# Scores of the short branch as three one-pass products of split q and k

## The reference: one layer with two attention branches

```
h = rms_norm(x, norm_g)                       # x: 1 x 4096 x 1024, float32
qa, ka, va, za, qb, kb, vb, zb, ga, gb = split(h @ w_in)
qa, ka = partial_rope(qa), partial_rope(ka)   # first 16 of 64 channels of a head
ya = swa_sink_attention(qa, ka, va, sinks) * silu(za)      # 8 q heads, 2 kv heads
yb = chunked_relpos_attention(qb, kb, vb, bias) * silu(zb) # 8 heads
merged = sigmoid(ga + b0) * (ya @ w_br_a) + sigmoid(gb + b1) * (yb @ w_br_b)
out = rms_norm(x + merged @ w_out, final_g)
```

## Time and profile before

| | us |
|---|---|
| median of 3 runs | 3419.65 (3418.62 to 3423.51) |
| the profiled execution, its own time | 3421.02 |
| its span in the profile | 3419.2 |
| TensorE busy | 3342.8 (98%) |
| VectorE busy | 1482.7 (43%) |
| ScalarE busy | 1422.4 (42%) |
| GpSimd busy | 1309.1 (38%) |
| mean granted TensorE clock | 0.999 |

### The profile page before, as it was taken

How to read it: one execution, slowest core, us unless ns; L and a number is a source line. 1 busy time by engine, 2 the same in 40 slices (tenths; PEclk the granted TensorE clock), 3 DMA queues, 4 the chain that set the end, 5 groups by cost and what they waited for, 6 DMA issues and landing times.

```text
span 3419.2 us, 48305 instructions
## 1 busy us (share of the span) xinstructions
PE 3342.8 (98%) x16328; PEld 2496.7 (73%) x16328; DVE 1482.7 (43%) x3097; ACT 1422.4 (42%) x2969; POOL 1309.1 (38%) x1087
## 2 busy tenths in 40 slices
PE   7999999999999999999999999999999999999998
PEld 6667876678766787667876678766787667876676
DVE  4662355513555135551355513555135551355512
ACT  4443444434444344443444434444344443444432
POOL 3334542344423454234542345423454234542244
PEclk9999999999999999999999999999999999999999
DMA  4212431124311242112421225211242112521123
GB/s 156 62 62 88 171 99 50 62 87 167 99 51 62 86 169 97 55 61 83 173 93 55 61 83 173 93 56 62 81 172 94 56 61 83 173 94 55 56 82 116
DMA packets 97782, 319.53 MB, mean 93 GB/s; under 512 B 9984, under 2 KB 26624, under 8 KB 95360
## 3 DMA queue, kind: packets, MB, share of 16 engines
q1 hardware_dynamic: 97536, 316.34, 28.5%
HBM read 299.52 MB, written 16.78 MB: 93 GB/s over the span
## 4 chain that ended last, share of the span: by engine, by line
PE 84%; issue 7%; DVE 5%; POOL 2%; ACT 1%; DMA 0%; DVEq 0%; POOLq 0%; SPq 0%; ACTq 0%
PE acc L909 16%; PE acc L911 14%; PE acc L910 14%; PE ps_o L1004 6%; PE ps_pt L973 5%; PE sc L953 3%; PE sc L909 3%; PE sc L911 3%; PE sc L910 3%; POOL w_lo L755 2%; PE sc L944 2%; PE sc L853 2%; PE sc L852 2%; PE sc L851 2%; PE sc L876 1%
## 5 line engine op out<-in xcount | busy, mean ns | idle before, releaser
L755 POOL TENSOR_TENSOR w_lo<-w_raw,w_hi 128x512 fp32r<-128x512 f32 x928 | 1210.3, 1310 | 2048.1 <-ACT w_hi L1058 2046.9
L909 PE MATMUL acc<-h_hi,w_hi 128*128 128x512 f32 x2432 | 1012.1, 416 | 15.5 <-DVE q L1316 15.5
L911 PE MATMUL acc<-h_hi,w_lo 128*128 128x512 f32 x2432 | 953.1, 392 | 0.0
L910 PE MATMUL acc<-h_lo,w_hi 128*128 128x512 f32 x2432 | 950.4, 391 | 0.0
L1058 ACT ACTIVATE w_hi<-w_raw 128x512 fp32r<-128x512 f32 x928 | 574.4, 625 | 393.1 <-DMA w_raw<-w 118.0
L909 PEld LDWEIGHTS acc<-h_hi,w_hi 128*128 128x128 f32 x2432 | 456.4, 188 | 228.5 <-issue 146.5
L911 PEld LDWEIGHTS acc<-h_hi,w_lo 128*128 128x128 f32 x2432 | 456.4, 188 | 101.7
L910 PEld LDWEIGHTS acc<-h_lo,w_hi 128*128 128x128 f32 x2432 | 458.1, 188 | 75.4
L1146 ACT ACTIVATE probs_b<-sc,negm 128x640 f32<-128x640 f32 x256 | 202.9, 794 | 390.3 <-DVE negm L1263 390.2
L1153 ACT ACTIVATE probs_t<-ps_pt 128x512 f32<-128x512 f32 (+1 forms) x272 | 150.7, 554 | 264.7 <-PE ps_pt L973 264.7
L1288 DVE SCALAR_TENSOR_TENSOR part<-th,sc 128x512 f32<-128x512 f32 x64 | 43.9, 686 | 467.9 <-PE sc L911 467.7
(11 more groups left out here) (140 smaller groups left out, 3916.4 us busy)
## 6 DMA issues: line engine op xcount, KB each, us to landing
w_raw<-w SPq DMA_DIRECT2D x464, 512.0 KB, 3.5
rows<-x SPq DMA_DIRECT2D x36, 512.0 KB, 7.4
xt<-x_t SPq DMA_DIRECT2D x16, 1024.0 KB, 10.0
out<-rows SPq DMA_DIRECT2D x32, 512.0 KB, 2.8
x_in<-x SPq DMA_DIRECT2D x28, 512.0 KB, 5.5
cs<-rope_tab SPq DMA_DIRECT2D x8, 512.0 KB, 4.3
bias<-near SPq DMA_DIRECT2D x1, 1024.0 KB, 13.5
g_out<-final_g SPq DMA_DIRECT2D x1, 512.0 KB, 11.6
```

Of the source, the lines that this page charges most:

```text
L755: pool.tensor_tensor(w_lo[n % 2][:, c], w_raw[n % 2][:, c], w_hi[n % 2][:, c].bitcast(FP32), ALU.subtract).then_inc(w_split, 1)
L909: pe.matmul(dst[:, :], hi, src_hi[:, k, :], start=begin, stop=False)
L910: pe.matmul(dst[:, :], hi, src_lo[:, k, :], start=False, stop=False)
L911: mm = pe.matmul(dst[:, :], lo, src_hi[:, k, :], start=False, stop=end)
```

## The change

q and k of branch A are kept as a rounded part and a remainder, both float32r (`q_a_hi`, `q_a_lo`, `k_a_hi`, `k_a_lo`), and the scores are three products in place of one float32 product. The two heads alternate within each term. To make the parts, the rope gets two further operations: after the sum (`rope_sum`) ScalarE rounds it (`rope_split`), and in a new step `rope_out` VectorE subtracts (`rope_done`). The rotated sine part goes to a buffer of its own, `pre_rot`, and the sum stays in `pre`. `q` of branch B becomes the single buffer `q_b`; branch A's q and the input buffer `x_in1` share the last two slots of `th`.

```
 lead:
-             v[0], [*v[1], ("rope_in", 0)], v[2], [("rope", 0), *v[3]], [("turn_v", 0), *k4[0]], ...
+             [*v[0], ("rope_out_k", 0)], [*v[1], ("rope_in", 0)], v[2], [("rope", 0), *v[3]],
+             [("turn_v", 0), *k4[0], ("rope_out", 0)], ...
 fill:
             fill[at_ + 3] = [("rope", s), *fill[at_ + 3]]
+            fill[at_ + 4] = [*fill[at_ + 4], ("rope_out", s)]

 GpSimd, keep_k:
-  pool.tensor_copy(k_a[:, 0:P], k_a[:, BLK:BLK + P]).then_inc(kept, 1)
+  pool.tensor_copy(k_a_hi[:, 0:P], k_a_hi[:, BLK:BLK + P].bitcast(FP32))
+  pool.tensor_copy(k_a_lo[:, 0:P], k_a_lo[:, BLK:BLK + P].bitcast(FP32)).then_inc(kept, 1)

 TensorE, scores of branch A:
-  for hh in range(2):
-      rows_ = slice(HD * hh, HD * hh + HD)
-      mm = pe.matmul(score_tile(s, hh, t)[:, c:A_KEYS], q[n % 2][rows_, t * P:(t + 1) * P],
-                     k_a[rows_, t * P + c:t * P + A_KEYS], start=True, stop=True)
+  terms = ((q_a_hi, k_a_hi), (q_a_lo, k_a_hi), (q_a_hi, k_a_lo))
+  for i, (q_part, k_part) in enumerate(terms):
+      for hh in range(2):
+          rows_ = slice(HD * hh, HD * hh + HD)
+          mm = pe.matmul(score_tile(s, hh, t)[:, c:A_KEYS], q_part[rows_, t * P:(t + 1) * P],
+                         k_part[rows_, t * P + c:t * P + A_KEYS], start=i == 0, stop=i == 2,
+                         skip_group_check=True)

 ScalarE, steps rope and rope_k (it had nothing in them):
+  act.wait_ge(rope_sum, b * NROPE + (ROPE_NO[step] + 1))
+  if kind == "rope_k" and not first:
+      wait_kept(act, b, "keep_k", PAIRS - 1)
+  act.activation(roped(kind)[0], pre[:, :], ACT.Copy).then_inc(rope_split, 1)

 VectorE, steps rope and rope_k, then rope_out and rope_out_k:
-  dve.tensor_tensor(dst, bank(step)[:, :], cs[:, 1, :], ALU.mult).then_inc(free(step), 1)
+  dve.tensor_tensor(pre_rot[:, :], bank(step)[:, :], cs[:, 1, :], ALU.mult).then_inc(free(step), 1)
   ...
-  dve.tensor_tensor(dst, pre[:, :], dst, ALU.add).then_inc(rope_done, 1)
+  dve.tensor_tensor(pre[:, :], pre[:, :], pre_rot[:, :], ALU.add).then_inc(rope_sum, 1)
+  dve.wait_ge(rope_split, b * NROPE + (no + 1))
+  dve.tensor_tensor(lo, pre[:, :], hi.bitcast(FP32), ALU.subtract).then_inc(rope_done, 1)
```

More of the change, by code:

```diff
@@ L154, in block_plan @@
     lead += [*tile("k", 0), q[0], [*q[1], ("rope_in_k", 0)], q[2], [("rope_k", 0), *q[3]],
-             v[0], [*v[1], ("rope_in", 0)], v[2], [("rope", 0), *v[3]], [("turn_v", 0), *k4[0]], *k4[1:], *tile("q", 4)]
+             [*v[0], ("rope_out_k", 0)], [*v[1], ("rope_in", 0)], v[2], [("rope", 0), *v[3]], [("turn_v", 0), *k4[0], ("rope_out", 0)], *k4[1:], *tile("q", 4)]
     for t in range(TT):
@@ L383, in program @@
     v_b = sb("v_b", [P, 2 * TT, PAIRS * P])
-    k_a = sb("k_a", [P, P + BLK])
+    k_a_hi = sb("k_a_hi", [P, P + BLK], FP32R)
+    k_a_lo = sb("k_a_lo", [P, P + BLK], FP32R)
     v_a = sb("v_a", [P, 1 + TT, P])
-    q_at = off[0]
-    q = [sb(f"q{i}", [P, BLK]) for i in range(2)]
+    q_b = sb("q_b", [P, BLK])
     z0 = sb("z0", [P, BLK])
@@ L411, in program @@
     pre_hi = at("pre_hi", [P, BLK], FP32R, y_lo_at + 4 * BLK * 7)
+    pre_rot = at("pre_rot", [P, BLK], FP32, y_lo_at + 4 * BLK * 6)
     bias = sb("bias", [P, 9, A_KEYS])
     x_in0_at = off[0]
-    x_in = [sb("x_in0", [P, D]), at("x_in1", [P, D], FP32, q_at)]
+    x_in0 = sb("x_in0", [P, D])
     probs_a = [at("probs_a0", [P, TT, A_KEYS], FP32, pa_at), at("probs_a1", [P, TT, A_KEYS], FP32, x_in0_at)]
@@ L418, in program @@
     cs = sb("cs", [P, 2, BLK])
+    th_at = off[0]
     th = sb("th", [P, 2 * AHEAD, BLK])
+    late_at = th_at + 4 * BLK * (2 * AHEAD - 2)
+    q_a_hi = at("q_a_hi", [P, BLK], FP32R, late_at)
+    q_a_lo = at("q_a_lo", [P, BLK], FP32R, late_at + 4 * BLK)
+    x_in = [x_in0, at("x_in1", [P, D], FP32, late_at)]
     gate = sb("gate", [P, BLK])
@@ L490, in program @@
     rope_cos = sem("rope_cos")
+    rope_sum = sem("rope_sum")
+    rope_split = sem("rope_split")
     rope_done = sem("rope_done")
@@ L633, in ring, with roped @@
         return probs_t[(FIRST_TURN if first else TURN)[turn][0] % RING]
+    def roped(kind):
+        if kind.endswith("_k"):
+            return k_a_hi[:, P:P + BLK], k_a_lo[:, P:P + BLK]
+        return q_a_hi[:, :], q_a_lo[:, :]
     def wait_kept(eng, b, kind, s):
@@ L727, in _ @@
             pool.memset(mhalf[:, :], -0.5).then_inc(zeroed, 1)
-            pool.memset(k_a[:, 0:P], 0.0).then_inc(zeroed, 1)
             pool.memset(v_a[:, 0, :], 0.0).then_inc(zeroed, 1)
@@ L731, in _ @@
             pool.memset(v_b[:, 0:TT, :], 0.0).then_inc(zeroed, 1)
-            pool.wait_ge(zeroed, 5)
+            pool.wait_ge(zeroed, 4)
             def rsqrt(which, t, n, got, got_count, mid, done, count):
@@ L826, in _ @@
             turn_rstd(0)
-            pe.wait_ge(zeroed, 5)
+            pe.wait_ge(zeroed, 4)
             def token_products(b, n, c):
@@ L952, in scores @@
                             if lo < B_HALF:
-                                mm = pe.matmul(sc[hh][:, c, lo:B_HALF], q[n % 2][rows_, t * P:(t + 1) * P],
+                                mm = pe.matmul(sc[hh][:, c, lo:B_HALF], q_b[rows_, t * P:(t + 1) * P],
                                                k_b[rows_, s - PAIRS, t * P + c * B_HALF + lo:t * P + (c + 1) * B_HALF],
@@ L1106, in job_done @@
                 elif name == "q":
-                    act.activation(q[POS[idx] % 2][:, :], ps, ACT.Copy, scale=SCALE).then_inc(free(step), 1)
+                    act.activation(q_b[:, :], ps, ACT.Copy, scale=SCALE).then_inc(free(step), 1)
                 elif name == "v":
@@ L1131, in body @@
                             act.activation(v_b[:, TT + t, :], ps_v[t], ACT.Copy).then_inc(v_out[0], 1)
+                    elif kind in ("rope", "rope_k"):
+                        act.wait_ge(rope_sum, b * NROPE + (ROPE_NO[step] + 1))
+                        if kind == "rope_k" and not first:
+                            wait_kept(act, b, "keep_k", PAIRS - 1)
+                        act.activation(roped(kind)[0], pre[:, :], ACT.Copy).then_inc(rope_split, 1)
                     elif kind == "merge_hi":
@@ L1309, in body @@
                     elif kind in ("rope", "rope_k"):
-                        s = step[1]
                         no = ROPE_NO[step]
                         wait_full(dve, b, step)
-                        if kind == "rope_k" and not first:
-                            wait_kept(dve, b, "keep_k", PAIRS - 1)
-                        dst = k_a[:, P:P + BLK] if kind == "rope_k" else q[POS[s] % 2][:, :]
-                        dve.tensor_tensor(dst, bank(step)[:, :], cs[:, 1, :], ALU.mult).then_inc(free(step), 1)
+                        dve.tensor_tensor(pre_rot[:, :], bank(step)[:, :], cs[:, 1, :], ALU.mult).then_inc(free(step), 1)
                         wait_freed(dve, b, step)
                         dve.wait_ge(rope_cos, b * NROPE + (no + 1))
-                        dve.tensor_tensor(dst, pre[:, :], dst, ALU.add).then_inc(rope_done, 1)
+                        dve.tensor_tensor(pre[:, :], pre[:, :], pre_rot[:, :], ALU.add).then_inc(rope_sum, 1)
+                    elif kind in ("rope_out", "rope_out_k"):
+                        hi, lo = roped(kind)
+                        no = ROPE_NO[(kind.replace("_out", ""), step[1])]
+                        dve.wait_ge(rope_split, b * NROPE + (no + 1))
+                        dve.tensor_tensor(lo, pre[:, :], hi.bitcast(FP32), ALU.subtract).then_inc(rope_done, 1)
                     elif kind == "scores":
```

## The result

The changed kernel takes **3447.75 us** (median of 4 runs, 3447.62 to 3447.98) against 3419.39 us for the kernel before: ratio 1.0077, 95% interval 1.0061 to 1.0092. That is 28.4 us more; the forecast was 3441 us, 21.4 us more than the 3419.65 us that it started from. The direction and the two waits came out as forecast. A third loss, about 11 us, was in no term of the sum: the granted clock.

What follows compares the result with a forecast made beforehand. TensorE, with work for 98% of the span, was taken as the bound. Lead 15.0 + q2's rope 8.0 + q1 and q3 0.4 - score step 1.5 = +21.9 us on 3419.65 gave 3441 us, range 3421 to 3487.

Steps and rivals of the forecast that it cites:

- the two waits: TensorE waiting for `turned` at v's turning, +1.87 us a block, and before the long branch's scores, +1.0 us a block.
- TensorE's step: Short branch's 128 score steps: three one-pass products paced by weight loads, -0.012 us a step, -1.5 us in all.
- the switch: Entry to TensorE's score group from products of another shape: change of shape, not precision, costs, so drain and entry stay.
- Both far ends of that bound: Score step: drain and exposed loads vanish, -50 us (rival, 7%); narrow products stream at four cycles a column, +82 (rival, 11%).
- the prediction's 0.56 us: Score step's three terms if loads overlap only across row groups: 3 x (0.11 + 0.08), +0.13 us a step, weighed little.
- Side by side: Score products of two heads on two row halves run together; rival that they no longer do: +40 us, 3483 us, 6%.
- The lead: Start of each block: longer key and q0 ropes delay `turned`, so TensorE turns v 1.87 us later, +15.0 us.
- q2's rope: ScalarE waits at q2's rope step, delaying exponentials and the long branch's next scores: +1.0 us a block, +8.0 us.
- q1 and q3: Ropes of q1 and q3: 1 us delay meets no TensorE instruction due over 0.1 us before its data; +0.4 us.
- the forecast's own range: Whole kernel: 3428 us (9.1 + 0 - 1.5) to 3452 us (all terms at their upper end), given 56%.
- waits of the other ropes: Upper bound for the ropes' waits: up to 0.3 us each, for each of 24 ropes.

Runs made afterwards that it cites:

- experiment 4: Branch A scores as one float32 product of the rounded parts: in the changed kernel 3449.37 us; in that kernel with v's turning and q2's rounding later 3423.99 us.
- g_one: Changed kernel with v's turning and q2's rounding moved later, keeping only the first of three products of a branch A score: 3391.79 us.
- g_b3: Changed kernel with v's turning and q2's rounding moved later, branch B's scores also as three one-pass products, without splitting its q and k: 3398.67 us.
- g_hh: Changed kernel with v's turning and q2's rounding moved later, head 0's three products ahead of head 1's instead of alternating: 3420.30 us.
- e1_fill: Changed kernel with eight additional one-pass products on TensorE between tile v0 and the turning of v, into an unused bank: 3439.46 us.
- e3_late2: Changed kernel with ScalarE's rounding of the rotated q2 moved behind the exponentials of (5, 2): 3439.23 us.
- e8_f32: Changed kernel with branch A's scores as one float32 product of the rounded parts alone, products with a remainder left out: 3449.37 us.

## Why the prediction was right, point by point

- **TensorE's step, -1.5 us:** right. -1.7 us by the timeline, 1.9 in experiment 4. The pace of a term is that of its load (g_one, 0.115 us against 0.11), the change of precision has no part in the switch, and one-pass products on 64 rows stream near one cycle a column (g_b3, 0.14 us for 320 columns). Both far ends of that bound, -50 and +82, are excluded. The group's 0.51 us leave no room for loads and streams of one half that take turns: the prediction's 0.56 us for three such terms and the 0.09 us behind them would be 0.65 us. The Trainium skill (TensorE: Matmul & The Clock Gate, Part 3) says in one place that loads overlap running products only on another row group, and the 0.65 us is the estimate by that rule, so this trace does not agree with it. The Trainium skill (TensorEngine Tiling, Key Properties) says that a change of tiling mode drains the array. This trace agrees: the gaps of 0.33 and 0.34 us stayed.
- **Side by side:** right in size. The alternating order, which I later took for its condition, is none: g_hh.
- **The lead, +15.0 us of wait:** 13.9 (19.4 - 5.5). Each step of the block that was worked out came within about 0.1 us (v is turned at 894.09, by the forecast at 887.33 + 6.87 = 894.20).
- **q2's rope, +8.0 us:** 7.2 (10.8 - 3.6), confirmed by moving one instruction.
- **q1 and q3, +0.4 us:** nothing is to be seen.
- **The step that failed:** the lead's price, "+1.87 us a block, +15.0 us", counted the wait alone. I had read the clock row as constant and had waits of 1.7 us without a dip beside it, and did not ask what 2.5 us in one piece would do. It cost 11 us more, 1.6 us for a dip in seven of eight blocks (8 products in 3.4 us at 0.43 us instead of 15 at 0.23), as e1_fill shows, which fills the idle time and keeps the rope's tail as it is. The sum of the terms was 21.9, the terms measured 13.9 + 7.2 - 1.7 = 19.4. With the clock's 11.0, and with 2.8 us less of other waits and 1.0 less of other products, that gives the profile's 26.6. The medians are 28.4 apart, which the spread of the runs before (3418.62 to 3423.51) allows for.
- **What was luck:** 3447.75 us lies in the forecast's own range of 3428 to 3452 although a term of 11 us was missing. Its upper end stood for waits of the other ropes, and these did not come.
- **Slips that change no chance:** 3419.65 + 21.9 is 3441.5, and the own range, by the terms it names, runs from 3427 to about 3450.

## What to carry to other kernels

Splitting a float32 product into three one-pass products paid here where the moving side takes longer to stream than a weight load of 0.11 us: 320 columns gained 0.21 us a group, 192 columns 0.01 us. A wait on the critical engine can cost more than its length: those up to 1.7 us cost their length alone, those from 1.8 us on mostly brought the clock down as well, 1.6 us more each time. So write down the longest idle stretch that a forecast makes and look for one of that length in the trace. And when an operation joins a chain that an in-order engine serves, its place in that engine's list counts more than its duration: 0.63 us of rounding in each of 8 blocks cost about 25 us at one place (14 of wait, 11 of clock) and nothing some lines further down.

## What was not expected of the hardware

- 2.44 us of idling brought the clock down to 1.2 GHz for 3.4 us in 7 of 8 cases in one execution and 5 of 8 in two others; 1.8 us did it too, at the start of the execution (e1_fill, e3_late2).
- The dip often comes after the work has begun again: 0.6 to 1.4 us behind the end of the wait in the changed kernel, 0.9 to 1.4 in e3_late2. In e8_f32 four of the five begin 0.1 to 0.5 us before it ends, so a full busy share beside a low clock is common, but not the rule.
- Two heads on the two halves of the rows ran side by side though three products of one stood ahead of the other's in the program (0.52 us a group, 0.51 alternating).
